# Expert loop of a hybrid token mixer with MoE: down product issued one slot behind gate and up

## The reference, cut to what matters

```python
def hier_moe(h, rg_w, rg_b, re_w, re_b, wg, wu, wd):
    ...
    gates = jnp.sum(jax.nn.one_hot(ids, N_EXPERTS, dtype=jnp.float32) * w_e[..., None], axis=-2).astype(h.dtype)
    y = jnp.zeros_like(h)
    for e in range(N_EXPERTS):
        hid = jax.nn.silu(h @ wg[e]) * (h @ wu[e])
        y = y + gates[..., e:e + 1] * (hid @ wd[e])
    return y
```

## Time and profile before

| | us |
|---|---|
| median of 3 runs (lowest, highest) | 1094.55 (1093.82, 1095.35) |
| span of the profiled execution | 1087.6 |
| TensorE busy | 898.1 |
| VectorE busy | 750.3 |
| ScalarE busy | 415.2 |
| GpSimd busy | 374.9 |
| expert loop: first gate matmul to last down matmul | 540.5 to 1030.7 |

### The profile page before, as it was taken

The page is one execution under the profiler, slowest core; times in us unless marked ns, Lnnn a source line. Parts: engine busy times, 40 slices in busy tenths (PEclk is TensorE's granted clock), DMA queues, the critical chain, the costliest instruction groups (busy, mean ns, idle before and its releaser), DMA issues.

```text
span 1087.6 us, 12479 instructions
## 1 busy us (share of the span) xinstructions
PE 898.1 (83%) x3689; PEld 630.0 (58%) x3690; DVE 750.3 (69%) x890; ACT 415.2 (38%) x520; POOL 374.9 (34%) x181
## 2 busy tenths in 40 slices
PE   6789999569898989992279998999999899988900
PEld 2354444224345468882268886888888677776700
DVE  2235999997993353446885768567655988888658
ACT  1333535125445221114142445335514555555312
POOL 1000806600000000002254637266241777766671
PEclk9999999789899999995589998999999888889955
DMA  8884413306214513316556748475462888887494
GB/s 319 290 329 155 139 36 96 96 1 207 82 41 163 224 58 116 116 78 233 192 188 238 270 162 305 189 270 212 162 244 77 305 319 304 324 319 281 153 362 198
DMA packets 108564, 213.48 MB, mean 196 GB/s; under 512 B 11006, under 2 KB 47996, under 8 KB 108540
## 3 DMA queue, kind: packets, MB, share of 16 engines
q1 hardware_dynamic: 97996, 174.37, 44.2%
q0 software_dynamic: 5904, 21.50, 5.5%
q10 hardware_dynamic: 4640, 17.30, 3.9%
HBM read 180.12 MB, written 33.03 MB: 196 GB/s over the span
## 4 chain that ended last, share of the span: by engine, by line
PE 47%; DVE 34%; issue 8%; DMA 4%; DVEq 4%; ACT 3%; SPq 0%; POOL 0%; ACTq 0%; POOLq 0%
DVE WP L1519 7%; PE bank L696 7%; DVE macc L1327 5%; PE bank L903 3%; PE bank L881 3%; PE bank L883 3%; PE bank L882 3%; PE bank L904 3%; PE bank L905 3%; PE bank L809 3%; PE bank L810 3%; PE bank L811 3%; DVE rkt L1533 2%; PE bank L678 2%; DVE fb L1643 2%
## 5 line engine op out<-in xcount | busy, mean ns | idle before, releaser
L616 POOL TENSOR_TENSOR WP<-raw,WP 128x1024 fp32r<-128x1024 f32 x64 | 186.7, 2947 | 0.7 <-ACT WP L1133 0.5
L696 PE MATMUL bank<-hT,wring 128*128 128x512 f32 x384 | 168.5, 597 | 2.6 <-ACT hT L961 1.9
L1519 DVE TENSOR_TENSOR WP<-raw,WP 128x2048 fp32r<-128x2048 f32 x62 | 156.8, 2569 | 11.3 <-ACT WP L1129 8.2
L1129 ACT ACTIVATE WP<-raw 128x2048 fp32r<-128x2048 f32 x64 | 119.5, 1917 | 89.8 <-issue 76.6
L881 PE MATMUL bank<-WP,xp 128*128 128x512 f32 x368 | 143.9, 391 | 1.5 <-DVE xp L1556 1.5
L883 PE MATMUL bank<-WP,xp 128*128 128x512 f32 x368 | 143.8, 391 | 0.0
L882 PE MATMUL bank<-WP,xp 128*128 128x512 f32 x368 | 143.6, 390 | 0.0
L696 PEld LDWEIGHTS bank<-hT,wring 128*128 128x128 f32 x384 | 73.4, 192 | 93.5 <-issue 90.1
L628 POOL TENSOR_TENSOR WP<-raw,WP 128x2048 fp32r<-128x2048 f32 x2 | 9.0, 4536 | 300.4 <-ACT WP L1129 300.4
L612 POOL TENSOR_TENSOR held<-held 128x1 f32<-128x1 f32 x24 | 36.2, 1509 | 218.1 <-DVE idg L1548 210.5
L1327 DVE SCALAR_TENSOR_TENSOR macc<-mring,silu_c,macc 128x256 f32<-128x256 f32 x112 | 88.7, 792 | 4.0
(11 more groups left out here) (278 smaller groups left out, 1478.3 us busy)
## 6 DMA issues: line engine op xcount, KB each, us to landing
raw<-in_expert_w_gate SPq DMA_DIRECT2D x64, 512.0 KB, 3.9
raw<-in_expert_w_up SPq DMA_DIRECT2D x64, 512.0 KB, 6.3
raw<-in_expert_w_down SPq DMA_DIRECT2D x64, 512.0 KB, 7.2
mring<-in_mod_w SPq DMA_DIRECT2D x20, 1024.0 KB, 5.0
expert_rows<-ysc ACTq DMA_DIRECT2D x23, 512.0 KB, 7.3
expert_rows<-g SPq DMA_DIRECT2D x16, 512.0 KB, 11.4
wring<-in_w_in SPq DMA_DIRECT2D x12, 512.0 KB, 5.9
mslot<-in_mod_w SPq DMA_DIRECT2D x4, 1024.0 KB, 14.7
```

Of the source, the lines that this page charges most:

```text
L616: pool.tensor_tensor(WP[:, j, 1, 2 * D:], raw[:, j, 2 * D:], WP[:, j, 0, 2 * D:].bitcast(F32), ALU.subtract).then_inc(s_lod[j], 1)
L696: mm = pe.matmul(o_, wring[:, n % 3, k, :], src, start=k == 0, stop=k == KD - 1)
L1129: A_(WP[:, j, 0, 0:2 * D], raw[:, j, 0:2 * D], ACT.Copy).then_inc(s_hgu, 1)
L1519: tt(WP[:, j, 1, 0:2 * D], raw[:, j, 0:2 * D], WP[:, j, 0, 0:2 * D].bitcast(F32), ALU.subtract).then_inc(s_logu[j], 1)
```

## The change

TensorE's loop is shifted by one step. Gate and up of slot 0, its hidden transpose and the row transposes of slot 1 are taken out in front of the loop; down of the last slot comes behind it. Iteration q issues gate and up of slot q+1, the row transposes of slot q+2, the slot numbers of q+3, down of slot q, and the hidden transpose of slot q+1. All other engines are written in the same shift. ScalarE in iteration q: copies of gate and up chunks 0 and 1 (if slot q+1 is a last one), tanh of slot q+1, row copies of q+2, gate and up chunks 2 and 3, down copies (if slot q is a last one), hidden copy of q+1, store of y of slot q. VectorE: split of chunk 0, hidden tile of q+1, row splits of q+2, slot numbers of q+3, splits of chunks 1 to 3, scaling of y of slot q, low part of the hidden tile of q+1, tables of q+4. GpSimd: gather of q+3, down splits (if slot q is a last one). The sync engine's program does not change.

Smaller parts: the hidden tile is transposed into bank 7 alone, copied and split in one instruction each instead of two; the routing weights keep a column for each slot; the last slot's y goes through `xg`; the semaphores of the first memsets are joined into one.

```diff
             def gather(q):
                 pool.wait_ge(s_ids, q + 1)
                 if not isinstance(q, int):
-                    hold(q - 2)
+                    hold(q - 3)
...
+            pool.wait_ge(s_xgt, 4)
+            gather(2)
             with pool.Fori(0, MAXT // 2) as it:
                 for par in range(2):
-                    with pool.If(2 * it + par < W):
-                        s = 2 * it + par
-                        L = pool.value_load(tab[0:1, 2, bass.ds(s, 1)], min_val=0, max_val=1)
-                        E1 = pool.value_load(tab[0:1, 0, bass.ds(s + 1, 1)], min_val=0, max_val=NE - 1)
-                        pool.wait_ge(s_xgt, 2 * s + 4)
-                        gather(s + 2)
+                    with pool.If(2 * it + par + 1 < W):
+                        q = 2 * it + par
+                        L = pool.value_load(tab[0:1, 2, bass.ds(q, 1)], min_val=0, max_val=1)
+                        E = pool.value_load(tab[0:1, 0, bass.ds(q + 1, 1)], min_val=0, max_val=NE - 1)
+                        pool.wait_ge(s_xgt, 2 * q + 6)
+                        gather(q + 3)
                         with pool.If(L > 0):
                             for j in range(KE):
-                                split_down(E1, j)
+                                split_down(E, j)

...
+            def turn_hidden(s):
+                pe.wait_ge(s_hid, 2 * s + 2)
+                for j in range(KE):
+                    mm = pe.transpose(bank[7][:, j * P:(j + 1) * P], sg[:, j * P:(j + 1) * P], ident)
                 mm.then_inc(s_hT, 1)

             def down(s, E, j):
                 pe.wait_ge(s_lod[j], E + 1)
-                if j % 2 == 0:
-                    pe.wait_ge(s_hps, 2 * s + j // 2 + 1)
                 if j == 0:
+                    pe.wait_ge(s_hps, s + 1)
                     pe.wait_ge(s_ye, 2 * s + 2)
...
+            pe.wait_ge(s_xgr, 2)
+            for j in range(KE):
+                gate_up(0, 0, j)
+            turn_rows(1, 0)
+            turn_rows(1, 1)
+            slot_numbers(2, pe.value_load(tab[0:1, 0, 2:3], min_val=0, max_val=NE - 1))
+            turn_hidden(0)
             with pe.Fori(0, MAXT // 2) as it:
                 for par in range(2):
-                    with pe.If(2 * it + par < W):
-                        s = 2 * it + par
-                        E = pe.value_load(tab[0:1, 0, bass.ds(s, 1)], min_val=0, max_val=NE - 1)
-                        E2 = pe.value_load(tab[0:1, 0, bass.ds(s + 2, 1)], min_val=0, max_val=NE - 1)
-                        pe.wait_ge(s_xgr, 2 * s + 2)
-                        gate_up(E, par, 0)
-                        gate_up(E, par, 1)
-                        gate_up(E, par, 2)
-                        gate_up(E, par, 3)
-                        turn_rows(s + 1, 0)
-                        turn_rows(s + 1, 1)
-                        turn_hidden(s, 0)
-                        turn_hidden(s, 1)
-                        slot_numbers(s + 2, E2)
+                    with pe.If(2 * it + par + 1 < W):
+                        q = 2 * it + par
+                        E0 = pe.value_load(tab[0:1, 0, bass.ds(q, 1)], min_val=0, max_val=NE - 1)
+                        E1 = pe.value_load(tab[0:1, 0, bass.ds(q + 1, 1)], min_val=0, max_val=NE - 1)
+                        E3 = pe.value_load(tab[0:1, 0, bass.ds(q + 3, 1)], min_val=0, max_val=NE - 1)
+                        pe.wait_ge(s_xgr, 2 * q + 4)
                         for j in range(KE):
-                            down(s, E, j)
+                            gate_up(E1, 1 - par, j)
+                        turn_rows(q + 2, 0)
+                        turn_rows(q + 2, 1)
+                        slot_numbers(q + 3, E3)
+                        for j in range(KE):
+                            down(q, E0, j)
+                        turn_hidden(q + 1)
+            for j in range(KE):
+                down(W - 1, NE - 1, j)


...
+            def early_hi(s, E1):
+                for j in range(2):
+                    act.wait_ge(s_gud, 4 * s + j + 1)
+                    hi_gate_up(E1, j)
+
+            def late_hi(s, E1):
+                act.wait_ge(s_gud, 4 * s + 4)
+                for j in range(2, KE):
+                    hi_gate_up(E1, j)
+
+            def tanh_and_rows(s, nxt):
+                act.wait_ge(s_gate, s + 1)
+                A_(sg[:], bank[0][:], ACT.Tanh, scale=0.5).then_inc(s_sg, 1)
+                for r in range(2):
+                    hi_rows(s + 1, nxt, r)
+
+            def hidden_hi(s):
+                act.wait_ge(s_hT, s + 1)
+                A_(hp[:, 0], bank[7][:].rearrange("p (k n) -> p k n", n=P), ACT.Copy).then_inc(s_hfr, 1)
+
+            L0 = act.value_load(tab[0:1, 2, 0:1], min_val=0, max_val=1)
+            E1 = act.value_load(tab[0:1, 0, 1:2], min_val=0, max_val=NE - 1)
+            with act.If(L0 > 0):
+                early_hi(0, E1)
+            tanh_and_rows(0, 1)
+            with act.If(L0 > 0):
+                late_hi(0, E1)
+            hidden_hi(0)
             with act.Fori(0, MAXT // 2) as it:
                 for par in range(2):
-                    with act.If(2 * it + par < W):
-                        s = 2 * it + par
-                        L = act.value_load(tab[0:1, 2, bass.ds(s, 1)], min_val=0, max_val=1)
-                        E1 = act.value_load(tab[0:1, 0, bass.ds(s + 1, 1)], min_val=0, max_val=NE - 1)
-                        with act.If(L > 0):
-                            for j in range(2):
-                                act.wait_ge(s_gud, 4 * s + j + 1)
-                                hi_gate_up(E1, j)
-                        act.wait_ge(s_gate, s + 1)
-                        A_(sg[:], bank[0][:], ACT.Tanh, scale=0.5).then_inc(s_sg, 1)
-                        for h in range(2):
-                            act.wait_ge(s_hT, 2 * s + h + 1)
-                            A_(hp[:, 0, 2 * h:2 * h + 2, :],
-                               bank[(7, 0)[h]][:, h * 2 * P:(h + 1) * 2 * P].rearrange("p (k n) -> p k n", n=P),
-                               ACT.Copy).then_inc(s_hfr, 1)
-                        for r in range(2):
-                            hi_rows(s + 1, 1 - par, r)
-                        with act.If(L > 0):
-                            act.wait_ge(s_gud, 4 * s + 4)
-                            for j in range(2, KE):
-                                hi_gate_up(E1, j)
+                    with act.If(2 * it + par + 1 < W):
+                        q = 2 * it + par
+                        L0 = act.value_load(tab[0:1, 2, bass.ds(q, 1)], min_val=0, max_val=1)
+                        L1 = act.value_load(tab[0:1, 2, bass.ds(q + 1, 1)], min_val=0, max_val=1)
+                        E1 = act.value_load(tab[0:1, 0, bass.ds(q + 1, 1)], min_val=0, max_val=NE - 1)
+                        E2 = act.value_load(tab[0:1, 0, bass.ds(q + 2, 1)], min_val=0, max_val=NE - 1)
+                        with act.If(L1 > 0):
+                            early_hi(q + 1, E2)
+                        tanh_and_rows(q + 1, par)
+                        with act.If(L1 > 0):
+                            late_hi(q + 1, E2)
+                        with act.If(L0 > 0):
                             for j in range(KE):
-                                act.wait_ge(s_dd, 4 * s + j + 1)
+                                act.wait_ge(s_dd, 4 * q + j + 1)
                                 hi_down(E1, j)
-                        act.wait_ge(s_ye, 2 * s + 4)
-                        act.dma_start(y_d[bass.ds(s, 1)].rearrange("a p d -> (a p) d"),
+                        hidden_hi(q + 1)
+                        act.wait_ge(s_ye, 2 * q + 4)
+                        act.dma_start(y_d[bass.ds(q, 1)].rearrange("a p d -> (a p) d"),
                                       ysc[:, par, :]).then_inc(s_ys[par], 16)
+            act.wait_ge(s_ye, 2 * W + 2)
+            act.dma_start(y_d[bass.ds(W - 1, 1)].rearrange("a p d -> (a p) d"), xg[:]).then_inc(s_ysl, 16)

...
             with dve.Fori(0, MAXT // 2) as it:
                 for par in range(2):
-                    with dve.If(2 * it + par < W):
-                        s = 2 * it + par
-                        L = dve.value_load(tab[0:1, 2, bass.ds(s, 1)], min_val=0, max_val=1)
-                        E1 = dve.value_load(tab[0:1, 0, bass.ds(s + 1, 1)], min_val=0, max_val=NE - 1)
-                        with dve.If(L > 0):
-                            lo_gate_up(E1, 0)
-
-                        dve.wait_ge(s_sg, s + 1)
-                        stt(out=sg[:], in0=sg[:], scalar=1.0, in1=bank[0][:], op0=ALU.add,
-                            op1=ALU.mult).then_inc(s_sil2, 1)
-                        dve.wait_ge(s_sil2, s + 1)
-                        dve.wait_ge(s_gud, 4 * s + 4)
-                        for h in range(2):
-                            hs = slice(h * 2 * P, (h + 1) * 2 * P)
-                            tt(sg[:, hs], bank[1][:, hs], sg[:, hs], ALU.mult).then_inc(s_hid, 1)
```

(81 more changed lines are left out.)

40 lines of the change are left out of this document (19 added, 21 removed).

## The result

| | before | after |
|---|---|---|
| median, us (lowest to highest) | 1094.18 (1090.58 to 1095.35), 4 runs | 1129.16 (1126.52 to 1131.61), 4 runs |
| ratio to before | 1 | 1.0327, 95% interval 1.0302 to 1.0353 |
| span of the profiled execution | 1087.6 | 1124.8 |
| TensorE busy | 898.1 | 879.3 |
| VectorE busy | 750.3 | 715.8 |

The changed kernel is 3.3% slower, 35 us. Every engine is busy for less time and the kernel is longer: the new time is waiting.

What follows compares the result with a forecast made beforehand. TensorE bounds the loop up to slot 15; afterwards a closed ring of load waits would. Front 840.5, release 860.5, six 32.4 us turns to 1054.9, last down 1070.0 (+39.1), end +1: span 1127.7, plus 6.95 gives 1134.6 us; range 1114 to 1148.

Steps and rivals of the forecast that it cites:

- The front, up to slot 15's gate and up: Loop until slot 15's gate and up end: one down fewer and shorter waits take 14.4 us off, to 840.5.
- The first release: Split of expert 8's down weights done, letting the next loads go: 20 us behind 840.5, at 860.5.
- The turn: Late single-slot experts, from one release of loads to the next: 32.4 us against 23.8; six make 194.4.
- The landing of chunk 1: From the release of the loads until ScalarE can copy gate and up chunk 1: 9.4 us, bounds 8.0 to 11.
- The last splits: Expert 15's down splits and last down, behind the last release at 1054.9: 15.1 us, ending at 1070.0.
- The end: Behind the last down: same work, but the fx load shares the DMA engines with y's last store, +1 us.
- The ring: From slot 14 on, gate and up loads wait in a closed chain for earlier down splits, 32.4 us per expert.
- the signs: Expected profile: last seven slots load four down, then eight gate/up; releases 32.4 us apart, hidden waits, lower clock; earlier pitch 18.9.
- (d): Late slots: the hidden transpose is still waited for, some 6 to 9 us per slot; inside the forecast, no own chance.
- Rival (a): Late slots: the ring does not close, VectorE holds the pitch at 22.9 us, kernel faster at 1077; chance 0.07.
- Rival (b): Late slots: the ring closes but GpSimd's hold and gather run uncontended, 28.4 us a turn, kernel 1111; chance 0.08.
- the 1123 of the gather alone: Late slots, by the Trainium skill: VectorE does not slow the gather's issue, turn 1.9 us shorter, kernel 1123 us.

Runs made afterwards that it cites:

- the experiment with the slot numbers: Kernel before, with TensorE issuing the slot numbers ahead of the two hidden transposes instead of behind them: 1093.7 us, ratio 1.0009.
- the first two experiments: Changed kernel, gate/up loads of e+1 ahead of down of e: 1051.24 us; kernel before, gate/up loads of e waiting for e-1's last down split: 1173.77 us.
- the first experiment: Changed kernel with the sync engine issuing gate and up loads of expert e+1 ahead of down of expert e: 1051.24 us, ratio 0.9615.

## Why the prediction was right

The forecast was 1134.6, the result 1129.16. By its steps:

- **The front, up to slot 15's gate and up.** Forecast 840.5, measured 829.1 (its gate and up starts at 817.94 and takes 11.18). I took the pitch of an undisturbed slot as unchanged, since the same instructions are issued. It fell by 0.85 us, some 12 us in 14 slots, which covers the 11.4. The term I did not have is the way over the hidden split, which I had priced at nothing; the experiment with the slot numbers shows that it is in series in the kernel before. Slot 5's wait, the slow down behind it and the small waits went as forecast, slot 0's stayed (6.6 us).
- **The first release.** Forecast 20 us behind, measured 21.3 (850.44).
- **The turn.** Forecast 32.4, measured 33.4 (six turns from 850.44 to 1051.04, 200.6 us). The links behind the landing were right as a sum to 0.1 us: from chunk 1's copy at 927.78 to the release at 950.72 it is 22.9, and 23.0 in my sum. The landing of chunk 1 took 10.6 us and not 9.4. Of the missing 1.2 us, 0.5 lie between the end of the last down load's issue and the first gate load's (917.22 to 917.73), and 0.25 in the issue of the four loads of chunks 0 and 1 (2.17 us, 1.92 in the reference that I used); what the rest is stays open. The value lies inside my bounds of 8 to 11.
- **The last splits.** Forecast 15.1 us from the last release to the last down, measured 12.2 (1063.26). The four splits took 9.41 us there, with none of VectorE's weight splits beside them, where I put in 11.65.
- **The end.** Forecast 1 us more than before, measured 4.7 (61.5 for 56.8 us behind the last down). 2.9 of it is VectorE reaching the last scaling late, behind tables that nobody reads and an idle 3.35 us that the profile puts down to "issue"; with the tables left out it follows at once. I had not looked at what is queued ahead of the peeled instruction. The rest, 1.8 us, is the fx load in front of the last store; I had the mechanism and too small a size.

The ring was forecast by its mechanism. That the total lies so close is partly luck, since the errors cancel: -11.4 in the front and -2.9 at the last splits against +1.3, +6.2 and +3.7. The span came out 2.9 below the forecast one. The other 2.6 us are in the last step: I added 6.95 us between span and median, and in the result they are 4.4 us apart.

Of the signs, four down loads are followed at once by eight gate and up loads, as forecast, but six times and not in each of the last seven slots. The hidden waits there are 9.3 to 11.3 us, more than the 6 to 9 under (d), and the granted clock of a late turn is 0.80 where it was 0.86. The pitch before slot 15 is 18.0 and not 18.9.

Rival (a), the ring does not close, fell with the first two experiments and with the load times; its time was wrong too. It had VectorE holding the pitch at 22.9 us, and with the ring open a slot takes 19.9. VectorE's busy time in such a slot is 18.6, not 21.1. The difference is in two operations that meet GpSimd's splits in both kernels: the split of chunk 0 took 4.48 us and takes 2.97, the small one at L1533 took 1.40 and takes 0.39, while GpSimd's four splits went from 11.65 to 13.7. I had taken all of the 21.1 as VectorE's own need. Rival (b), an uncontended GpSimd, is refuted by hold and gather at 2.30 and 2.85 us, as in the kernel before. Its time had a slip: the first release has a gather of its own, so 4.0 us come off seven times and not six (1107 and not 1111), and the same holds for the 1123 of the gather alone (1121). By what the Trainium skill's "SBUF — State Buffer", section "Who interferes with whom", infers, the gather should have been near its lone 0.97 us; the measurement decides, and it is 2.84 or 2.85 in every turn. The Trainium skill's "DMA: Bandwidth & Descriptors", opening table, puts the HBM limit per core at about 358 GB/s; the first experiment's window has 363 GB/s of reads and writes together, close to it, and does not settle the difference to the 393 GB/s from the spacing of chunks 1 and 3.

## What to carry to other kernels

When a loop is software-pipelined on one engine, follow every buffer that its instructions free, and what the freeing releases in queues that nobody edits. A load queue served strictly in order is part of the schedule: here its order was right for the old loop, wrong for the new one, and exchanged in both it was right for the new one only. Sum the ring from release to release; if engines and DMA are all below two thirds and the pitch still grows, look for it first.

## What I had not expected of the hardware

- Four down splits on GpSimd (128x1024 fp32 each) took 9.41 us with none of VectorE's weight splits beside them, 11.62 in the changed kernel's turn, where VectorE's splits run mostly ahead of them, and 14.39 when they met three of VectorE's weight splits. Those three took 6.70 us in the changed kernel and 8.90 where they met GpSimd's.
- Eight tiny matmuls took TensorE 1.07 us behind the transposes of the hidden tile and 0.35 us behind the row transposes. No run here shows why.
- A gather of 0.5 MB issued together with 4 MB of weight loads put the start of the first weights' copy back by 2.5 us (7.4 to 10.0 us behind the first gate load).
